# Stick-breaking attention in a two-layer trunk: the order of the query rows, the values in two halves, the output copy and the scan buffers

## The reference

```python
def sb_attend(q, q_pos, k, v, k_pos):
    z = jnp.einsum('bqhd,bkhd->bhqk', q, k) * (SB_HEAD_DIM ** -0.5)
    mask = (k_pos[None, :] < q_pos[:, None])[None, None]
    log_keep = jnp.where(mask, jax.nn.log_sigmoid(-z), 0.0)
    suffix = lax.cumsum(log_keep, axis=3, reverse=True) - log_keep
    a = jnp.where(mask, jnp.exp(jax.nn.log_sigmoid(z) + suffix), 0.0)
    return jnp.einsum('bhqk,bkhd->bqhd', a, v)
```

## Time and profile before

| | |
|---|---|
| time, median of 3 runs | 3015.72 us (3013.76 to 3016.24) |
| the profiled execution's own time | 3013.41 us |
| its span | 3011.3 us |
| stick-breaking stage, first scores to last values | 1781.43 to 2087.3 us |
| one body of it, steady | 75.2 us |
| TensorE busy, share of the span | 96% |
| mean granted TensorE clock | 0.98 |

### The profile page before, as it was taken

The page is one execution under the profiler, slowest core; times in us unless marked ns, Lnnn a source line. Parts: engine busy times, 40 slices in busy tenths (PEclk is TensorE's granted clock), DMA queues, the critical chain, the costliest instruction groups (busy, mean ns, idle before and its releaser), DMA issues. The chain is left out here.

```text
span 3011.3 us, 41450 instructions
## 1 busy us (share of the span) xinstructions
PE 2880.0 (96%) x15811; PEld 2505.5 (83%) x15811; DVE 1164.1 (39%) x1782; ACT 949.0 (32%) x1924; POOL 618.1 (21%) x478
## 2 busy tenths in 40 slices
PE   7989997899999999999899989997999999999998
PEld 6878885688998899989798865555898899889997
DVE  5656662443332233224311027776442233223323
ACT  4344543321221122113222238886231122112212
POOL 3100000121211122112121225555021121112211
PEclk9989998899999999999899999998999999999999
DMA  4311103401111011110235365553110111101111
GB/s 139 89 48 42 44 30 98 175 22 42 57 49 35 28 56 49 34 42 29 94 127 177 103 160 143 142 135 117 51 57 31 33 56 49 35 28 56 49 35 77
DMA packets 188026, 215.48 MB, mean 72 GB/s; under 512 B 17280, under 2 KB 148864, under 8 KB 187904
## 3 DMA queue, kind: packets, MB, share of 16 engines
q1 hardware_dynamic: 187904, 213.82, 23.5%
HBM read 166.17 MB, written 47.61 MB: 71 GB/s over the span
## 5 line engine op out<-in xcount | busy, mean ns | idle before, releaser
L1485 DVE TENSOR_TENSOR x<-m_ps,x 128x512 f32<-128x512 f32 x324 | 223.9, 691 | 607.0 <-PE m_ps L76 607.0
L1521 DVE TENSOR_TENSOR m_sq<-m_relu 128x384 f32<-128x384 f32 x192 | 170.7, 889 | 505.0 <-ACT m_relu L1417 505.0
L74 PE MATMUL m_ps<-h_h,m_up0h 128*128 128x384 f32 x768 | 257.0, 335 | 0.0
L76 PE MATMUL m_ps<-h_h,m_up0l 128*128 128x384 f32 x768 | 256.7, 334 | 0.0
L75 PE MATMUL m_ps<-h_l,m_up0h 128*128 128x384 f32 x768 | 256.7, 334 | 0.0
L74 PE MATMUL m_ps<-h_h,m_up1h 128*128 128x384 f32 x768 | 256.5, 334 | 0.0
L75 PE MATMUL m_ps<-h_l,m_up1h 128*128 128x384 f32 x768 | 256.5, 334 | 0.0
L76 PE MATMUL m_ps<-h_h,m_up1l 128*128 128x384 f32 x768 | 256.5, 334 | 0.0
L1417 ACT ACTIVATE m_relu<-m_ps 128x384 f32<-128x384 f32 x192 | 94.5, 492 | 507.2 <-PE m_ps L76 507.2
L1412 ACT CAST m_dn0h<-m_dn_raw 128x1024 fp32r<-128x1024 f32 x16 | 16.8, 1051 | 547.6 <-PE m_ps L76 547.5
L2304 POOL TENSOR_TENSOR e_b<-e_b,e_r 128x128 f32<-128x128 f32 (+7 forms) x128 | 155.0, 1214 | 129.5 <-DVE e_r L2357 129.5
(11 more groups left out here) (494 smaller groups left out, 7174.0 us busy)
## 6 DMA issues: line engine op xcount, KB each, us to landing
m_up_raw<-in_mlp_w_up SPq DMA_DIRECT2D x64, 512.0 KB, 4.6
m_dn_raw<-in_mlp_w_down SPq DMA_DIRECT2D x64, 512.0 KB, 3.4
h_raw<-scratch_oT SPq DMA_DIRECT2D x4, 1536.0 KB, 15.1
scratch_qr<-a_qrst SPq DMA_DIRECT2D x9, 512.0 KB, 3.4
a_x<-in_x_prompt SPq DMA_DIRECT2D x8, 512.0 KB, 4.9
b_qr<-scratch_qr SPq DMA_DIRECT2D x4, 1024.0 KB, 7.0
scratch_oT<-b_o SPq DMA_DIRECT2D x32, 128.0 KB, 1.7
new_p_sb_k<-d_rows SPq DMA_DIRECT2D x16, 256.0 KB, 2.0
```

The lines of the kernel that those rows point to most:

```text
L74: pe.matmul(out, w[0], m[0], start=start, stop=False)
L76: return pe.matmul(out, w[1], m[0], start=False, stop=stop)
L1485: dve.tensor_tensor(x[:, t, cols], bank[:, 4 + n % 3, :], x[:, t, cols], ALU.add).then_inc(added.sem, 1)
L1521: dve.tensor_tensor(sq[n % 2][:], relu[n % 2][:], relu[n % 2][:], ALU.mult).then_inc(sq_done.sem, 1)
```

## The change

The order of the steps in a pair becomes short row, long row: a group has the query tiles s and 7 - s of both heads (s = 0 to 3), so that any two steps have 9 blocks together. Since the two tiles of a group see different numbers of keys, only the first s + 1 blocks are multiplied with both, 256 columns; the others, 7 - 2s of them, with the long tile alone, 128 columns. So the memset of e_pt goes, and e_pt holds the pairs of blocks first and the long row's upper blocks behind them. The values of a group go in two parts instead of four, after the first transposes of every second step. The first part takes the blocks that ACT copies and waits for ACT alone, the second takes those that DVE copies and waits for DVE. ACT copies the output at the end of the third step after the group, where it was in the middle of the fourth. There are four scan buffers, two short and two long, and a scan waits for the product of step n - 4. The store of an output goes to two pieces of 128 columns in place of one of 256.

```diff
     VALUES_LAG = 4
+    VALUES = ((0, 4, 8), (0, 3, 7), (0, 2, 6), (0, 2, 5))
...
         m = n % SbSchedule.PAIR_STEPS
-        return n // SbSchedule.PAIR_STEPS % 2, m // 2 % 2, 2 * (m // 4) + m % 2
+        short = m // 4
+        return n // SbSchedule.PAIR_STEPS % 2, m // 2 % 2, NPT - 1 - short if m % 2 else short
+
+    @staticmethod
+    def turns(n):
+
+        q = SbSchedule.where(n)[2]
+        return [range(k, min(k + 4, q + 1)) for k in range(0, q + 1, 4)]
...
-        scanned, weighted = signal("e_scan", 4), signal("e_weighted", 2)
+        scanned, weighted = signal("e_scan", 4), signal("e_weighted", 4)
...
         def turned_rows(n, task):
-            s0, at = task[0][1], (n % 2) * P
-            return pt[n // 2 % 4][:, s0:s0 + len(task), at:at + P]
+            x, n_blocks = pt[n // 2 % 4], len(task)
+            if task[0] >= NPT // 2:
+                return x[:, NPT // 2 + task[0]:NPT // 2 + task[0] + n_blocks, :]
+            first = 2 * task[0] + n % 2
+            return x[:, first:first + 2 * n_blocks - 1:2, :]
+
+        def turned_block(g, a, k, wide):
+            x = pt[2 * (g % 2) + a]
+            if k >= NPT // 2:
+                return x[:, NPT // 2 + k, :]
+            return x[:, 2 * k:2 * k + 2, :].rearrange("p s c -> p (s c)") if wide else x[:, 2 * k + 1, :]
...
-                sp.dma_start(scratch["oT"][2 * i + g // 4, :, cols], o_st[g % 4][:]).then_inc(
+                short, tall = g % 4, NPT - 1 - g % 4
+                rows = scratch["oT"][2 * i + g // 4, :, 0:SEQ].rearrange("p (q c) -> p q c", c=P)
+                sp.dma_start(rows[:, short:tall + 1:tall - short], o_st[g % 4][:]).then_inc(
                     o_out[g % 4].sem, 16)
...
-                    if j == 0 and values_of is not None and values_of % 4 == 3:
-                        output(i, values_of // 4)
+                if values_of is not None and values_of % 4 == 2:
+                    output(i, values_of // 4)
...
-                weighted.wait(dve, S.STEPS * i + n - 1)
+                weighted.wait(dve, S.STEPS * i + n - 3)
...
-            def values(i, g, quarter):
-                if quarter == 0:
-                    for u in range(2):
-                        t_out[u].wait(pe, TURNS[u] * i + copies(S.before(4 * g + 4), u))
+            def values(i, g, half):
+                blocks = S.VALUES[short]
+                t_out[half].wait(pe, TURNS[half] * i + copies(S.before(4 * g + 4), half))
+                if half == 0:
...
-                for k, slot in order[len(order) * quarter // 4:len(order) * (quarter + 1) // 4]:
+                for k in range(blocks[half], blocks[half + 1]):
+                    cols = slice(0 if k <= short else P, GQ)
...
-                    if j == 0 and values_of is not None:
-                        values(i, values_of // 4, values_of % 4)
+                    if j == 0 and values_of is not None and values_of % 2 == 0:
+                        values(i, values_of // 4, values_of % 4 // 2)
```

51 lines of the change are left out of this document (26 added, 25 removed).

## The result

The changed kernel takes **2971.4 us** (median of 4 runs, 2970.0 to 2972.8), the kernel before 3015.7 (4 runs, 3013.8 to 3016.2). The ratio is 0.9856, with a 95% interval of 0.9844 to 0.9868: 44.3 us less, where 28.6 were forecast. The direction and the mechanism were right; the size was not.

A forecast was written before the change was run, and what follows sets the result against it. PE, busy for 96% of the span, was taken as the bound. Visits -15, values' work -7.0, waits -9.6 and start +3 sum to -28.6 from 3013.4: 2984.8, plus 2.3 for the median, 2987.1 us; range 2981 to 3004.

The forecast's parts named there:

- What bounds the kernel: Whole kernel: PE is busy for 96% of the span, so time falls only where PE's work or waits shrink.
- A visit costs 0.33 us: Each time PE turns to a block of values and back, it pays 0.33 us beside the values' own work.
- Half of the new visits go straight on to the sample's matmuls: Visits fall from 112 to 64: 48 x 0.33 = 15.8 us, taken as 15 because some exits were unpriced; bounds 12 to 17.
- The values' work: Value matmuls: 128-column pairs at 0.11 us, half a wide pair, bring the work from 70.4 to 63.4 us, 7.0 less.
- The waits, 13.6 to 4: PE's waits before the values: those on DVE's and output copies go, ACT's copy leaves 4 us; 9.6 us gained.
- Four scan buffers: DVE's scans: four buffers remove DVE's wait for POOL, but PE does not wait there, so they gain nothing.
- The start, +3: Stage's start: two 8-block rows stand first, step 4's transposes come 4.2 us later, 1.2 was paid afterwards before: +3 us.
- The end, nothing: Stage's end: it drains short rows instead of long ones, with its waits already in the 13.6; no separate term.
- The stores and loads, nothing: Output stores in two pieces land in 2.3 us, and the next pair's loads stay hidden behind 16 steps; no cost.
- a new wait at ACT's copy: Rival: PE waits 0.4 to 0.8 us for ACT in each of 32 groups; 2997 to 3009 us, chance 0.18.
- Narrow matmuls at the wide price: Rival: a 128-column value pair costs 0.22 us like a wide one; +28 us, about 3015, chance 0.06.
- the late long row: Rival: the long row's chain exceeds four steps and PE stops at 64 rows' transposes; at 1 us each 3051, chance 0.04.

The follow-up runs named there:

- the kernel with four visits: The changed kernel with a group's values in four visits again and the output copied a step later: 3010.2 us, ratio 0.9986.
- The two kernels that part visits and sample: The changed kernel with the visits moved to the long rows' steps, 2977.0 us; the changed kernel with the sample's pieces moved there instead, 2979.9 us.
- the kernel with the early signal: The changed kernel with the first pair's queries, keys and values signalled ahead of the cache's loads in SP's queue: 2969.6 us, ratio 0.9851.
- the odd steps: The changed kernel with its two visits moved from the short rows' steps to the long rows' steps, output copied one step later: 2977.0 us.

## Why the forecast was right in kind and off in size

Point by point, by the steps of the prediction:

- **What bounds the kernel: right.** PE did, and does. The saved PE time became time of the kernel, but only because the waits fell with it.
- **A visit costs 0.33 us: right for a visit that leads back to scores.** 0.34 by the kernel with four visits and by the starts. It was read at one place, which happened to be of that kind. The Trainium skill, "TensorEngine Tiling (Array Packing)", Key Properties, states that switching the tiling mode requires a drain, without a price. The 0.34 agrees with that, being what stands beside the values' own spacings.
- **"Half of the new visits go straight on to the sample's matmuls [...] and I can't price those exits from a like row, so I take 15": this is the step that failed.** It gave every visit the price of one that leads back to scores. Before, 16 of a body's 28 visits do, and after, none of the 16. Eight lead to the sample's transposes, at 0.30 us, and eight to its 32-column matmuls, at 0.24, which also removes the *sample's* own way out, 0.09 a piece. The two kernels that part visits and sample need 2.0 and 2.2 us of PE a body more, 8 to 9 us in the stage. Together with the visits' own part (12 a body at 0.34, 16.5 in the stage) the term comes to 25 us instead of 15. My bounds of 12 to 17 us were drawn about the price of one kind of exit and left no room for this.
- **The values' work, 7.0 less: right.** 6.8 by PE's matmuls; a narrow pair is 0.11 us, and 0.106 less than a wide one. The Trainium skill, "TensorE: Matmul & The Clock Gate", Part 3, The mechanism, says in its list that a weight load overlaps with matmuls in flight only when the row group differs, which would make a narrow pair dearer by 0.05 or more (the prediction's estimate). The 16 narrow matmuls in 1.09 us contradict it.
- **The waits, 13.6 to 4: nearly right** (2.8 left, at ACT's copies as said). Their size was right, their logic too simple: they are no term of their own beside the visits. In the kernel before, taking visits away made waits *grow*.
- **Four scan buffers, nothing: wrong, with no harm to the sum.** Without them the change gives 16.7 us less. I had asked whether PE waits there now, and not whether it would wait there once it is faster.
- **The start, +3: measured +4.35.** The first values came at 1797.8 instead of 1795, with a chain of 12.0 us from ACT's first sigmoid. The stage itself began 2.1 us later in that execution, so the first values are 2.8 us later than forecast, and 0.7 counted from the first scores. The longer half clock accounts for no more than some 0.6 us of it, by the kernel with the early signal.
- **The end, nothing: this was the second miss, 3.7 us.** I read only the end's waits. Yet the last part has other work in it: with the rows in alternation, the last body's scores have 6 chunks fewer in it and not 4, and from the last scores to the end of the last values it is 8.6 us and not 14.1, since the last group has 5 blocks to finish and not 8.
- **The stores and loads, nothing: right.** The stores land in 3.8 us instead of 2.3, and no one waits.

In sums for the stage: visits -16.5, their way back shared with the sample -8.5, the values' work -6.8, waits -10.8, the start +4.35. That makes -38.3 of the -43.2; the end's 3.7 leaves 1.2 us that I can't assign. The forecast's terms made -28.6: of the 14.6 us between, 8.5 are the shared switches, 3.7 the end, 1.5 the visits' own price, 1.2 the waits, 1.2 unassigned, less 1.35 for the start and 0.2 for the values.

Added up from the single starts instead, the visits with their exits and the sample's own switches fall by 5.3 us a body, 21 in the stage and not 25. Some 3 of the 4 us between are delays in before that are too short for the list of waits, and lie in PE's busy time: in a body, two score matmuls start 0.20 us behind a transpose instead of 0.03, one score matmul 0.51 behind the last instead of 0.34, and one transpose 0.25 behind the mask instead of 0.07. After has none of them. So it is in part luck that the forecast's terms meet the 65.66 of the odd steps so closely.

The rivals: a new wait at ACT's copy is there but is 0.3 us in 9 groups, not 0.4 to 0.8 in 32. Narrow matmuls at the wide price and the late long row did not come. What one of them described, a wait in the place of work, does exist, in every kernel that has only part of the change.

**What stays open.** The two kernels that part visits and sample show that the neighbourhood costs 2.0 to 2.2 us a body, with the same matmuls, and the starts show at which steps. They also show that it is not the number of weight columns as such: the turn's second transpose, with 16 weight columns (128*16), starts 0.11 us behind the first and pays nothing. Those that pay are the values, in two tiles side by side, and the sample's, in four. Why they pay is not shown: no kernel changed the tiles alone. Nor has any kernel the new order of the rows alone, so what the alternation is worth by itself is open too. So are the unassigned 1.2 us.

## What to carry to other kernels

On an in-order engine that bounds a stage, count its switches between kinds of work and not only the work: give each visit its way out and its way back, and look who stands beside it, since a neighbour with a switch of its own may share one. Time saved on such an engine is kept only as far as its suppliers are ready sooner; before pricing a saving, ask of every wait now hidden what it will be when the body is as short as you forecast, and do not count on one part alone: here two visits alone gave nothing. Price the ends of the stage by their work, what is left to drain, and not by their waits.

## What the chip showed that I had not expected

- Matmuls in the same number and of the same shapes took 63.6, 65.7 and 65.8 us of PE's busy time a body, by their order. Behind transposes, the values or the sample's 32-column matmuls start 0.20 us after the last one, and other transposes 0.11.
- The granted clock fell to half while PE waited for the loads, and stood there over the stage's first 9 us. With ACT busy for 11.3 of the 12.0 us up to the first values, 4.7 us less of it (early signal) shortened that stretch by 0.6 us only.
- A sigmoid ahead of ACT's first wait took the table's load (1.28 us) off ACT's way to its first sigmoid, and the first values came 0.6 us sooner.
- Two scan buffers instead of four made DVE wait for POOL 52 times, 57.2 us in all (after: 7 times, 8.5 us), of which the kernel felt 16.7.
